# A hybrid decoder layer with PEER experts: 224 instead of 256 prompt tokens take their experts by row fetches

## The reference, cut to what matters

```python
u_rows = p['peer_u'][idx]
act = jax.nn.gelu(jnp.einsum('phkd,pd->phk', u_rows, xb).astype(jnp.float32))
coef = (gates * act).astype(xb.dtype)
return jnp.einsum('phk,phkd->pd', coef, p['peer_v'][idx])
```

## Time and profile before

| | us |
|---|---|
| median of 3 runs (lowest, highest) | 4481.94 (4481.36, 4485.39) |
| the profiled execution's own time | 4479.3 |
| its span | 4477.5 |
| PE busy in the span | 3768.5 (84%) |
| VectorE (DVE) busy | 2996.9 (67%) |
| GpSimd (POOL) busy | 2085.3 (47%) |
| ScalarE (ACT) busy | 1478.9 (33%) |
| HBM read, written | 1047.54 MB, 40.40 MB |

### The profile page before, as it was taken

The page is one execution under the profiler, slowest core; times in us unless marked ns, Lnnn a source line. Parts: engine busy times, 40 slices in busy tenths (PEclk is TensorE's granted clock), DMA queues, the critical chain, the costliest instruction groups (busy, mean ns, idle before and its releaser), DMA issues. The chain is left out here.

```text
span 4477.5 us, 65816 instructions
## 1 busy us (share of the span) xinstructions
PE 3768.5 (84%) x24298; PEld 3495.9 (78%) x24298; DVE 2996.9 (67%) x4531; ACT 1478.9 (33%) x1891; POOL 2085.3 (47%) x1162
## 2 busy tenths in 40 slices
PE   6877989999996898977688999898898888877777
PEld 3337888889885897977588988888888788777777
DVE  5777654555553224997877877777677777777776
ACT  5664344344342114223233333222222222222222
POOL 2343222222223233325366777666666676556562
PEclk9988999999996898989889999999999999999998
DMA  8972222222221222213399999999999999999994
GB/s 311 358 299 68 73 68 80 76 81 72 70 76 53 83 96 104 80 59 141 138 358 390 411 412 394 388 364 372 354 394 386 394 394 392 375 339 358 355 373 154
DMA packets 253130, 1090.63 MB, mean 244 GB/s; under 512 B 25352, under 2 KB 78856, under 8 KB 172296
## 3 DMA queue, kind: packets, MB, share of 16 engines
q1 hardware_dynamic: 167440, 543.60, 32.7%
q0 software_dynamic: 73728, 536.90, 29.8%
q10 hardware_dynamic: 11776, 7.52, 0.5%
HBM read 1047.54 MB, written 40.40 MB: 243 GB/s over the span
## 5 line engine op out<-in xcount | busy, mean ns | idle before, releaser
L247 POOL TENSOR_TENSOR wlo<-raw,whi 128x1024 fp32r<-128x1024 f32 x551 | 1342.2, 2443 | 1352.0 <-ACT whi L243 1346.5
L243 ACT CAST whi<-raw 128x1024 fp32r<-128x1024 f32 x672 | 698.8, 1051 | 1298.3 <-DMA raw<-in_u 495.4
L262 PE MATMUL gps<-hi_d,whi 128*128 128x320 f32 x2048 | 662.1, 323 | 174.0 <-POOL wlo L247 153.5
L2091 PE MATMUL gps<-chi,whi 128*128 128x320 f32 x2048 | 659.4, 322 | 158.8 <-POOL wlo L247 70.3
L262 PE MATMUL gps<-lo_d,whi 128*128 128x320 f32 x2048 | 652.1, 318 | 0.0
L262 PE MATMUL gps<-hi_d,wlo 128*128 128x320 f32 x2048 | 651.5, 318 | 0.0
L2091 PE MATMUL gps<-clo,whi 128*128 128x320 f32 x2048 | 645.9, 315 | 0.0
L2091 PE MATMUL gps<-chi,wlo 128*128 128x320 f32 x2048 | 645.6, 315 | 0.0
L2178 DVE SCALAR_TENSOR_TENSOR dps<-ring,coef,dps 128x2048 f32<-128x2048 f32 x252 | 592.0, 2349 | 4.8
L2165 DVE CUSTOM_DVE_ANT_0 ring<-ring,dps 128x2048 f32<-128x2048 f32 x256 | 582.5, 2280 | 0.0
L262 PEld LDWEIGHTS gps<-hi_d,whi 128*128 128x128 f32 x2048 | 402.5, 197 | 194.3 <-POOL wlo L247 168.3
(11 more groups left out here) (388 smaller groups left out, 6110.7 us busy)
## 6 DMA issues: line engine op xcount, KB each, us to landing
raw<-in_u SPq DMA_DIRECT2D x256, 512.0 KB
raw<-in_v SPq DMA_DIRECT2D x256, 512.0 KB
wada<-in_w_ada SPq DMA_DIRECT2D x96, 1024.0 KB, 6.5
raw<-in_w_in SPq DMA_DIRECT2D x96, 512.0 KB
gateD<-gst SPq DMA_DIRECT2D x8, 2560.0 KB, 7.5
gate<-gateD SPq DMA_DIRECT2D x32, 640.0 KB
raw<-in_w_out SPq DMA_DIRECT2D x32, 512.0 KB
raw<-in_w_q SPq DMA_DIRECT2D x32, 512.0 KB
```

The costliest lines, as they stand in the source:

```text
L243: act.copy(whi[:, k.slot, :], raw_of(k)).then_inc(W.hi, 1)
L247: pool.tensor_tensor(wlo[:, k.slot, :], raw_of(k), whi[:, k.slot, :].bitcast(F32), ALU.subtract).then_inc(W.lo, 1)
L262: m = pe.matmul(gps[:, bank, 0:DT], w, x[:, kt, :], start=(kt == 0 and n == 0), stop=(kt == KT - 1 and n == 2))
L2091: m = pe.matmul(gps[:, 2 + dt, 0:DT], w[:, slot, cols], x[:, buf, c, :], start=(c == 0 and n == 0), stop=(c == NG - 1 and n == 2))
```

## The change

`SPT` becomes 224: tile 0 keeps 128 rows, tile 1 has 96 (`ROWS`). `DT` becomes 352, `GB` 44. The ring has five buffers instead of six (`RING`), three of them before the expert stage (`RING0`); the second buffer of `ga` and the fourth of `raw` move to the room that is freed. Every fetch of a tile 1 and every operation of VectorE on it covers 96 partitions. The calls of `next_row()` stay where they were in phase b; in phase a they are spread, half behind each of the two halves. `next_row()` now counts the calls in `due`, and a v row (n >= 256) is fetched `LAG` = 2 calls later than the ring would allow.

```diff
-SPT = 256
-NST = SPT // P
+SPT = 224
+NST = -(-SPT // P)
+ROWS = [min(P, SPT - t * P) for t in range(NST)]
 DT = T - SPT
-GB = 40
+GB = 44
 NGB = DT // GB
-RING = 6
-RING0 = 4
+RING = 5
+RING0 = 3
+LAG = 2
...
             pool.indirect_dma_start(
-                out=rings[row_slot[n]][:, :], out_offset=None, in_=src,
-                in_offset=bass.IndirectOffsetOnAxis(ap=spi[:, tile % NST, j:j + 1], axis=0)
+                out=rings[row_slot[n]][0:ROWS[tile % NST], :], out_offset=None, in_=src,
+                in_offset=bass.IndirectOffsetOnAxis(ap=spi[0:ROWS[tile % NST], tile % NST, j:j + 1], axis=0)
             ).then_inc(w_row[row_slot[n]], 16)
...
                     for k in range(3):
+                        last = ROWS[NST - 1]
+                        pe.transpose(gps[:, k, 0:P - last], slots[last:P, NST - 1, k, :], ident[last:P, last:P])
                         for t in range(NCH - NST):
-                            pe.transpose(gps[:, k, t * CH:(t + 1) * CH], slots[:, NST + t, k, :], ident)
+                            o = P - last + t * CH
+                            pe.transpose(gps[:, k, o:o + CH], slots[:, NST + t, k, :], ident)
...
-                    fetched = [RING0]
+                    fetched, due = [RING0], [RING0 - RING]
 
                     def next_row():
-                        if fetched[0] < NSP:
-                            fetch(pool, fetched[0], S.taken)
+
+                        due[0] += 1
+                        n = fetched[0]
+                        if n < min(due[0] + RING - (LAG if n >= NSP // 2 else 0), NSP):
+                            fetch(pool, n, S.taken)
                             fetched[0] += 1
...
                     def A(g, buf, k, after):
                         for c in range(NG):
-                            for j in (2 * c + 2, 2 * c + 3):
+                            rows = rows_due((g - 2) // 2, g % 2 * NG + c)
+                            for n, j in enumerate((2 * c + 2, 2 * c + 3)):
                                 lo(k.plus(j) if j < 8 else after.plus(j - 8))
-                            for _ in range(rows_due((g - 2) // 2, g % 2 * NG + c)):
-                                next_row()
+                                for _ in range(rows // 2 if n else rows - rows // 2):
+                                    next_row()
...
-                        got = rings[row_slot[n]][:, :]
+                        mine = slice(0, ROWS[tile % NST])
+                        got, held = rings[row_slot[n]][mine, :], rows4[mine, :]
...
-                            act.activation(coef[:, :, :], udot[:, :, :], ACT.Gelu_apprx_tanh).then_inc(S.ugel, 1)
+                            for b in range(NST):
+                                act.activation(coef[0:ROWS[b], b, :], udot[0:ROWS[b], b, :],
+                                               ACT.Gelu_apprx_tanh).then_inc(S.ugel, 1)
```

More of the change, by code:

```diff
@@ L1601, in to_rows @@
                         for kt in range(KT):
-                            o = rows4[:, kt * P:(kt + 1) * P]
-                            pe.matmul(o, hi_s[:, kt, tile * P:(tile + 1) * P], identr[:, :], start=True, stop=False)
-                            m = pe.matmul(o, lo_s[:, kt, tile * P:(tile + 1) * P], identr[:, :], start=False, stop=True)
+                            o = rows4[0:ROWS[tile], kt * P:(kt + 1) * P]
+                            mine = slice(tile * P, tile * P + ROWS[tile])
+                            pe.matmul(o, hi_s[:, kt, mine], identr[:, :], start=True, stop=False)
+                            m = pe.matmul(o, lo_s[:, kt, mine], identr[:, :], start=False, stop=True)
                         m.then_inc((S.x0t, S.x1t)[tile], 1)
@@ L1659, in _ @@
                     act.wait_ge(S.x1t, 1)
[L1660 removed]
+                    act.copy(xrow[0:ROWS[1], :], rows4[0:ROWS[1], :]).then_inc(S.x1c, 1)
                     for c in range(EARLY * NG):
@@ L1892, in _ @@
                             dve.wait_ge(S.mm, i * QUADS + (2 * o + 2))
-                            m = compare(ga[:, o % 2], 0, tokens(i, o))
+                            m = compare(ga[o % 2][:, :, :], 0, tokens(i, o))
                             if o % 2:
@@ L1912, in build @@
         chi = sb("chi", [P, 2, NG, DT], F32R, at=at7)
[L1913 to L1916, removed]
+        level_at = [const_at + C_LEVEL * 4]
+        udot = sb("udot", [P, NST, H * TOPK], at=level_at)
+        coef = sb("coef", [P, NST, H * TOPK], at=level_at)
+        raws += [sb("raw2", [P, HALF], at=at7)[:, :], sb("raw3", [P, HALF], at=[spare_at])[:, :]]
         rings += [sb(f"ring{n}", [P, D], at=at7) for n in range(RING0, RING)]
@@ L2164, in take @@
                                 dve.wait_ge(S.xt, tile)
-                            m = dve.tensor_tensor_reduce(out=got, in0=got, in1=rows4, scale=1.0, scalar=0.0,
+                            m = dve.tensor_tensor_reduce(out=got, in0=got, in1=held, scale=1.0, scalar=0.0,
                                                          op0=ALU.mult, op1=ALU.add,
-                                                         accum_out=udot[:, tile, j:j + 1])
+                                                         accum_out=udot[mine, tile, j:j + 1])
                         else:
@@ L2170, in take @@
                             if n == NST * NSLOT:
-                                dve.wait_ge(S.ugel, 1)
-                                ch(dve.tensor_tensor(coef[:, :, :], coef[:, :, :], spg[:, :, :], ALU.mult))
-                            by = coef[:, t, j:j + 1]
+                                dve.wait_ge(S.ugel, NST)
+                                for b in range(NST):
+                                    c = coef[0:ROWS[b], b, :]
+                                    m = dve.tensor_tensor(c, c, spg[0:ROWS[b], b, :], ALU.mult)
+                                ch(m)
+                            by = coef[mine, t, j:j + 1]
                             dve.wait_ge(S.taken, n)
                             if j == 0:
-                                m = dve.tensor_scalar(rows4, got, by, None, ALU.mult)
+                                m = dve.tensor_scalar(held, got, by, None, ALU.mult)
                             else:
-                                m = dve.scalar_tensor_tensor(got if j == NSLOT - 1 else rows4, got, by, rows4,
+                                m = dve.scalar_tensor_tensor(got if j == NSLOT - 1 else held, got, by, held,
                                                              ALU.mult, ALU.add)
```

20 lines of the change are left out of this document (12 added, 8 removed).

## The result

The changed kernel takes 4759.52 us (median of 4 runs, 4754.14 to 4771.89) against 4481.65 for the kernel before in the same comparison: ratio 1.0624, 95% interval 1.0602 to 1.0647. It is 278 us slower where 42 us less were predicted, far outside the range.

The account below looks back on a forecast made before the run. DMA was taken to bound good u pairs, stalls and a circle of waits to slow the tile 1 parts. Terms 5 + 6 + 16 + 12 + 11 - 11 - 87 + 6 = -42 gave 4437 profiled, 4440 us median; range 4396 to 4484.

Parts of the forecast that it names:

- u tile 1: Expert stage, second u part, 8 pairs at 69.1 us: DMA no longer a bound, TensorE stalls stay, +1.4 a pair, +11 us.
- v tile 1: Expert stage, last v part, 7 pairs at 78.5 us: the circle goes, DMA bounds nothing, pairs of 66, -87 us.
- Rival 1: Tile 1 parts: 96-row fetches relieve nothing, DMA bounds of 62.5 and 68.0 us stay; +26, 4466 us; chance 0.08.
- A rule against it: Tile 1 fetches: partitions 0 to 63 and 64 to 127 use different ports, so 96 rows leave the even ports' bytes unchanged.
- u tile 0: Expert stage, first u part, 8 pairs at 65.0 us: bytes stay, TensorE work grows to 62.0, pairs of 66.5, +12 us.
- rival 5: Turns of TensorE's expert loops: six more instructions ahead may move the stalls, 26 us less or 60 more; chance 0.03.
- The circle: v tile 1, phase b: GpSimd's fetch waits for VectorE, VectorE for TensorE, TensorE for GpSimd's `wlo`; said to go with `LAG`.
- rival 4: v tile 1: the circle is not as thought, 16 us of idle stay, +39 instead of -87, 4566 us; chance 0.06.
- v tile 0: Expert stage, first v part, 7 pairs at 71.3 us: waits for halves shrink by about a third, pairs of 69.7, -11 us.
- Rival 2: v parts: rows fetched later land too late, 76.2 us a pair from 12.5 us delay, +46 in tile 0, 4486; chance 0.11.
- Products: TensorE's expert stage products: 352 columns take 161.3 ns, 14.7 more, so a pair has 62.0 us of work, +5.6.
- rival 3: Routing stage: products under 256 columns run slower, 224 columns take 187 ns, +63 us instead of 5, 4498; chance 0.07.

Follow-up runs that it names:

- The last experiment: The changed kernel with tile 1 fetches back at 128 rows and 24 small transposes added behind TensorE's gate loop: 4464.59 us, ratio 0.9957 against the kernel before.

## Why the prediction was wrong

**The step that failed** is the sentence on u tile 1 and v tile 1, "96-row fetches are 0.786 MB, a pair 21.7 MB or 52 us, no longer a bound". It divides the smaller bytes by the rate of full-width transfers. At the rate that 96-partition ones have with halves beside them, 270 GB/s, the pair takes 80 us, and the 23.5 MB of a v pair 87 instead of 57. The price is 255 us (4759.5 less 4504.3), some 120 in either tile 1 part; u tile 1 had +11 and got +94.

**Rival 1** ("96 rows relieve nothing") had the right place and the wrong far end. It was priced as no relief, 4466, and had 0.08. The bound from below the term was worked out (nothing saved), the one from above was missing: that fewer rows could cost more than all of them. The rule quoted under "A rule against it" fits the rows of 0–63 and 32–95, and would still have given 31 us for 96. No row of the kernel before had any width but 128. The reason given against the rival, that engines take turns over all packets, was not one.

**u tile 0** had +12 and got +62. Most of the rest is the stall, rival 5 in another form: the stall of u tile 1 went as it says (worth 37 us in the kernel before, not 26), but some 40 came in u tile 0, which it did not consider. Its count of six instructions was wrong as well; it left out the gate loop's longer body. Without the stall the part takes 533.3, +13, pairs of 66.7 where 66.5 was the value taken.

**v tile 1** had -87 and got +69. The circle was as explained: `LAG` with the spread takes TensorE's waits for `wlo` in phase b away and gives 51 us (549.4 to 498.2), and `LAG` alone is no worse there (70.2 us a pair), so rival 4 falls. The size was too large even with full fetches. With 18.3 fetches of 128 rows a pair needs 68 us of DMA, and all runs with `LAG`, 128-row fetches and no stall there end at 69.9 to 71.4, a little above it. The 66 taken presupposed the relief that did not come.

**v tile 0** had -11 and got +16 (with full fetches 510.7 to 513.8, +12 to +15). The term was mis-sized. The halves came sooner, as it says: with full fetches ScalarE waits 122 us for them instead of 246, at the longest 11.2 instead of 17.0. But the part got no shorter. Rival 2 has a share in that, VectorE now waits 26.7 us for rows, and the products are longer; how much is due to each, and what the ring of five does by itself, no run shows. 12.5 us of delay a row it is not: with the 128-row fetches all v parts stay below 76.2 a pair when no stall is in them.

**Products.** The series in the routing stage of the changed kernel (timeline, start and duration):

```profile
1899.86 0.27 PE L281 MATMUL gps<-hi_s,wlo 128*128 128x224 f32 x1
1899.96 0.33 PE L281 MATMUL gps<-hi_d,wlo 128*128 128x352 f32 x1
...
1903.68 0.26 PE L281 MATMUL gps<-lo_s,whi 128*128 128x224 f32 x1
1903.78 0.34 PE L281 MATMUL gps<-lo_d,whi 128*128 128x352 f32 x1
```

From the first 224-column start to the last are 3.82 us for 14 couples, 273 ns each, as predicted (266 + 7); 224 columns hold TensorE 0.10 us and not 0.187, so rival 3 falls. 352-column products of the expert stage start 0.16 us apart (predicted 161 ns). The gates take 174 us for 172. The end grew by 12 us instead of 6, and by 5 and 8 in the runs with full fetches and with 24 transposes.

**The sum as a whole** does not come out even without the two surprises. The last experiment has no 96-row fetch and no large stall, and its profile is 18 us under the one of the kernel before (spans 4459.0 and 4477.5), where the sum has 42. But the kernel before still has its stall. Against the kernel before with its loops moved (span 4443.1) it is 16 us longer: +15 at the start, +21 and +12 in the u parts, +15 and -55 in the v parts, +8 at the end. Only the later fetch pays, and the 32 tokens more cost more than that.

Two slips change nothing: in the earlier trace rows the engines are full from slice 20 on, counted from 0, not 22, and rival 2 with tile 1 comes to 4557 (7 x 10.2 more than 4486), not 4550.

**What beats both kernels.** The kernel before with `LAG` and the spread (4427), and with the moved loops as well: 4391.61 us, 2.0% less than before (interval 1.6 to 2.4%). Against this one the last experiment, with the loops at nearly the same place, is 73 us longer: with 128-row fetches, 32 tokens more in the dense products only add TensorE time (5.6 us a pair) and save no transfer. The ring of five may have a part in it.

## What to carry to other kernels

Before a transfer is made narrower to save bytes, measure its rate at that width and those partitions, with the traffic that it shares the engines with: a DMA share near 1 at a low GB/s is the sign. Where a worker takes instructions in order, put the one that waits for the latest event a step later; that was worth 0.8% by itself here, and 1.2% with the fetches spread. And when long loops stall at their turns without a releaser, any edit ahead of them, on the same engine, is also an experiment with their place: count its instructions, loop bodies included, and try a few places before the edit is judged.

## What the runs showed of the hardware that was not expected

- Twelve fetches of 8 KB a partition took 31.4 us on 128 partitions, 41.4 on 0–95, 37.2 on 32–127, 48.5 on 0–103, 56.9 on 0–119, 30.8 on 0–63 and 17.5 on 32–95. Only the last is clearly faster than the full width.
- Beside narrow fetches the loads take longer too, a packet of the plain queue 154 ns instead of 114; in the kernel of transfers the two together took about the sum of their own times (58.3 us for 41.4 and 16.3).
- TensorE's loops of 768 products (842 instructions, weight loads not counted) lost some 40 us over three turns in one place, 37 in another (552.9 against 515.9 for u tile 1), as much over twelve small waits in a third, and next to nothing in a fourth. A loop of four turns that stalled had 34 packets of instructions moved, one that did not had 6.
